# VectorE instead of Pool computes the lower weight parts during the selective scan of a hybrid decoder step

## What is computed

```python
def mamba_mixer(h, ssm_state, conv_state, in_w, conv_w, conv_b, dt_bias, a_log, d_skip, norm_w, out_w):
    z, xbc, dt = split(h @ in_w)
    xbc = silu(causal_conv(xbc, conv_w, conv_b))        # 4 taps
    xs, Bm, Cm = split(xbc)                             # 4 groups of 8 heads
    y, h_last = ssd_scan(xs * dt, dt * A, Bm, Cm, h0)   # chunks of 128 tokens
    y = (y + xs * d_skip) * silu(z)
    y = y * rsqrt(mean(y * y, by group) + eps) * norm_w
    return y @ out_w, h_last, new_conv
```

## Time and profile before

| | before |
|---|---|
| median of 3 runs | 2139.93 us (2133.59 to 2141.44) |
| profiled execution, its own time | 2141.42 us |
| its span in the trace | 2139.7 us |
| PE busy | 1987.8 us, 93% |
| VectorE, ScalarE, Pool busy | 38%, 33%, 45% |
| mean granted TensorE clock | 0.938 |
| chain of waits, by engine | PE 63%, issue 13%, DVE 9%, POOL 8%, ACT 5% |

### The profile page before, as it was taken

How to read it: one execution, slowest core, us unless ns; L and a number is a source line. 1 busy time by engine, 2 the same in 40 slices (tenths; PEclk the granted TensorE clock), 3 DMA queues, 4 the chain that set the end, 5 groups by cost and what they waited for, 6 DMA issues and landing times.

```text
span 2139.7 us, 36778 instructions
## 1 busy us (share of the span) xinstructions
PE 1987.8 (93%) x14824; PEld 1822.0 (85%) x14824; DVE 818.6 (38%) x1564; ACT 705.8 (33%) x1291; POOL 960.4 (45%) x685
## 2 busy tenths in 40 slices
PE   6989899979889998999999999989978999999997
PEld 5987887868788998999998998855547899999996
DVE  7373564746454210022233112267745622002134
ACT  4453553633133211122223113166634422112222
POOL 2445454454447532356453332344402565345552
PEclk9998999989998979999996998989999899999998
DMA  4211313122131216222221244350060122222221
GB/s 162 76 50 40 119 50 118 40 84 109 50 115 60 87 52 158 79 79 80 87 79 69 79 146 123 95 188 1 21 237 31 50 79 89 79 79 88 79 79 64
DMA packets 52629, 184.61 MB, mean 86 GB/s; under 512 B 7070, under 2 KB 11838, under 8 KB 50976
## 3 DMA queue, kind: packets, MB, share of 16 engines
q1 hardware_dynamic: 40272, 129.66, 18.3%
q0 software_dynamic: 9952, 50.08, 6.5%
q10 hardware_dynamic: 2288, 3.23, 0.4%
HBM read 166.59 MB, written 27.28 MB: 91 GB/s over the span
## 4 chain that ended last, share of the span: by engine, by line
PE 63%; issue 13%; DVE 9%; POOL 8%; ACT 5%; DMA 1%; ACTq 0%; POOLq 0%; SPq 0%; DVEq 0%
PE dense L1273 44%; POOL split L673 4%; PE dense L1596 3%; PE dense L1679 2%; PE dense L1636 1%; DVE tile L1815 1%; PE bS L1385 1%; PE bXM L1666 1%; POOL tile L767 1%; DMA o_sssm<-tile 1%; PE dense L1294 1%; POOL hid L792 1%; PE bXM L1447 1%; PE bXM L1392 1%; ACT tile L1111 1%
## 5 line engine op out<-in xcount | busy, mean ns | idle before, releaser
L1273 PE MATMUL dense<-xs,split 128*128 128x288 f32 x6848 | 987.0, 302 | 31.2 <-POOL split L673 9.1
L1273 PEld LDWEIGHTS dense<-xs,split 128*128 128x128 f32 x6848 | 950.4, 194 | 65.1 <-issue 45.4
L673 POOL TENSOR_TENSOR split<-ring,split 128x1024 fp32r<-128x1024 f32 x212 | 533.5, 2516 | 856.6 <-ACT split L919 834.5
L919 ACT ACTIVATE split<-ring 128x1024 fp32r<-128x1024 f32 x212 | 224.0, 1057 | 822.5 <-PE dense L1273 799.1
L1273 PE MATMUL dense<-hid,split 128*128 128x288 f32 x3072 | 416.7, 298 | 6.4 <-POOL split L673 6.4
L1273 PEld LDWEIGHTS dense<-hid,split 128*128 128x128 f32 x3072 | 415.1, 191 | 6.6 <-POOL split L673 6.6
L1827 DVE SCALAR_TENSOR_TENSOR tile<-tile,dense 128x576 f32<-128x576 f32 (+1 forms) x56 | 42.2, 754 | 421.7 <-PE dense L1273 421.7
L1997 DVE TENSOR_SCALAR sq<-dense 128x576 f32<-128x576 f32 x64 | 48.5, 758 | 310.4 <-PE dense L1273 310.4
L890 POOL TENSOR_SCALAR tile<-tile,tile,tile 128x128 f32<-128x128 f32 (+3 forms) x128 | 77.2, 617 | 81.4 <-DVE tile L2161 81.4
L1815 DVE SCALAR_TENSOR_TENSOR tile<-tile,tile,tile 128x512 f32<-128x512 f32 x72 | 87.6, 1217 | 42.4 <-ACT tile L1000 40.6
L792 POOL TENSOR_TENSOR hid<-sq,hid 128x576 f32 x64 | 76.9, 1202 | 0.0
(11 more groups left out here) (316 smaller groups left out, 2198.4 us busy)
## 6 DMA issues: line engine op xcount, KB each, us to landing
ring<-in_w SPq DMA_DIRECT2D x212, 512.0 KB, 3.3
tile<-in_state POOLq DMA_DIRECT2D x4, 2048.0 KB, 9.5
o_sssm<-tile POOLq DMA_DIRECT2D x4, 2048.0 KB, 7.5
tile<-in_cmp POOLq DMA_DIRECT2D x32, 256.0 KB, 3.2
tile<-in_win POOLq DMA_DIRECT2D x8, 1024.0 KB, 6.0
tile<-in_sel SPq DMA_DIRECT2D x32, 256.0 KB, 5.2
o_kv<-tile POOLq DMA_DIRECT2D x1, 3456.0 KB, 12.2
bskew<-bscr SPq DMA_DIRECT2D x1, 3072.0 KB, 23.0
```

Source lines behind the costliest of these rows:

```text
L673: pool.tensor_tensor(split[:, j, 1, :], ring[:, j, :], split[:, j, 0, :].bitcast(F32), ALU.subtract).then_inc(w_split, 1)
L919: act.activation(split[:, j, 0, :], ring[:, j, :], ACT.Copy).then_inc(w_hi, 1)
L1273: mm = pe.matmul(dense[:, 2 * par + h_, 0:HT], split[:, j, w, cols], v[:, kk, h_ * HT:(h_ + 1) * HT], start=kk == 0 and t == 0, stop=kk == ...
```

## The change

From the first tile on VectorE makes the lower parts of the scan. A stands behind the convolution (and norm, and residual) of its tile and ahead of the wait for y (`y_done`). B stands in the next tile, behind the mask L1878 and ahead of the product L1883; for the last tile it stands behind the loop. Each has a wait for `w_hi`, the first one also a wait until Pool has done its own 12. Pool gets one new wait behind the scan, until VectorE has made its last lower part, ahead of its next one.

```diff
@@ gpsimd, in the tiles
                 if n + 1 < len(TILES):
                     segment_rows(*TILES[n + 1])
-                if filler(g, c):
-                    split_lo(filler(g, c)[0] + 2)
                 if c == 3:
...
                     if g + 1 < MG:
                         load_states(g + 1)
-                if filler(g, c):
-                    split_lo(filler(g, c)[1] + 2)
...
+            pool.wait_ge(w_split, S_OUT[1] + 2)
             finish_los(0)
@@ vector
+            def split_lo(s):
+                if s == GB + 2:
+                    dve.wait_ge(w_split, s)
+                dve.wait_ge(w_hi, s + 1)
+                j = s % NSLOT
+                dve.tensor_tensor(split[:, j, 1, :], ring[:, j, :], split[:, j, 0, :].bitcast(F32),
+                                  ALU.subtract).then_inc(w_split, 1)
+
+            def split_before(n):
+                if n and filler(*TILES[n - 1][:2]):
+                    split_lo(filler(*TILES[n - 1][:2])[1] + 2)
...
                 dve.tensor_tensor(Gm[0:L, 0:L], bM[0:L, P:P + L], triu[0:L, c // 4, 0:L], ALU.mult
                                   ).then_inc(g_masked, 1)
+                split_before(n)
                 dve.wait_ge(g_masked, n + 1)
...
                     residual(B_OUT[0], 2 * c - 2, ALPHA, filler(g, c)[0] + 1)
+                if filler(g, c):
+                    split_lo(filler(g, c)[0] + 2)
 
                 dve.wait_ge(y_done, n + 1)
...
                 if c == 0 and g:
                     mean_square(g - 1)
+            split_before(len(TILES))
             mean_square(MG - 1)
```

## The result

The changed kernel takes 2102.02 us (median; 2100.64 to 2109.36) beside 2139.47 us for the kernel before on the same chip: a ratio of 0.984 (95% interval 0.981 to 0.986), 37 us less; the slowest run after lies 24 us under the fastest before. The profiled execution took 2102.03 us, its span is 2100.3 us (2139.7 before), its mean granted clock 0.946 (0.938 before).

A forecast was written before the change was run, and what follows sets the result against it. TensorE's waits in the scan for VectorE and Pool chains, with VectorE blocked by Pool's lower part, were taken as the bound. Terms 6.8 + 6.5 + 2.1 + 4.8 + 3.6 + 1 = 24.8 us less gave 2115 us, range 2107 to 2128.

The forecast's parts named there:

- The mechanism: In the scan, VectorE's two-operand SBUF work stands still while Pool's lower part runs; a tap takes 2.96 instead of 0.75 us.
- the group starts: Starts of groups 1 to 3: TensorE's waits for xdec shrink without Pool's B ahead of it, 4.8 us gained.
- (3, 1): Tile 1 of group 3: the norm takes 3.0 instead of 5.87 us; minus A, 1.7 us gained.
- the ordinary ends: Four tile ends with no norm behind: each stall of 2.2 us shrinks by 1.7, 6.8 us gained.
- four times 1.62 us of clock: Behind the four ordinary tile ends' stalls the clock stays high, 6.5 us gained.
- The rival by which the lock stays with Pool's other work: Pool's other work blocks the taps instead, tile ends keep their 2.2 us stalls: 2132 us; chance 0.13.
- the rival of a clock that stays low: Behind the shortened stalls the clock stays low, 6.5 us less gain: 2121.5 us; chance 0.2.
- A as pure addition: Taps long for another reason, A adds 1.2 us at some 16 tile ends: 2154 us; chance 0.08 with late ScalarE.
- c = 4: Tiles with c = 4: A and Pool's first multiplication collide at y's sum; 0 to 4.8 us gained, 1 taken.
- (3, 3): Tile 3 of group 3: y's lower parts take 3.0 instead of 4.91 us, 1.9 us gained; clock left out, up to 1.6.
- the norm tiles: Tiles c = 3 of groups 1 and 2: stalls at both ends shrink, together 2.1 us gained.
- A wrong sign that I had named: A wait of VectorE for ScalarE's split ahead of A would show the forecast wrong.

The follow-up runs named there:

- e4: Changed kernel, with idle subtractions on Pool (about 2.1 us, result unread) at A's old place in all 19 tiles: 2146.95 us.
- e7: Kernel before, all lower parts still on Pool, but A moved behind the update of the state: 2112.3 us.
- e1: Changed kernel with only A on VectorE; B stays with Pool at its old place: 2124.57 us.
- e2: Changed kernel with only B on VectorE; A stays with Pool at its old place: 2131.35 us.
- e5: Changed kernel, with idle subtractions on Pool at A's old place in the four c = 4 tiles only: 2114.31 us.
- e3: Kernel before, with Pool making the scan's lower parts for 8 of 1024 columns only, the rest left out: 2080.64 us.
- e8: Changed kernel with A, in c = 4 only, behind the second of the eight states instead of ahead of y: 2094.38 us.
- e6: Changed kernel with A behind the state update in every tile, in c = 4 behind the second of the eight states: 2083.46 us.
- e13: e6 with the norm's products in the norm tiles of groups 1 and 2 made for 8 of 576 tokens only: 2074.2 us.
- e12: Changed kernel with the norm's products in the norm tiles of groups 1 and 2 made for 8 of 576 tokens only: 2091.89 us.

## Why the prediction was right, and where it was wrong

**The mechanism** was right for the tile ends, the group starts and (3, 1). The taps are short, the subtraction takes 1.22 us in the median on VectorE and 1.29 in the mean (forecast 1.2), the ordinary ends and (3, 1) came out within 0.7 us of their terms, and four times 1.62 us of clock came back. The rival by which the lock stays with Pool's other work fell: two taps of 2.4 us and a few of 1.5 remain in the scan, but none at the ends that count. So did the rival of a clock that stays low (window of 1.00 above) and that of A as pure addition (e4 has it: there A and a blocked tap stand together, and the time is a little above that of before). The Trainium skill's warning ("Perfetto Trace Analysis", Optimizing Scalar/DVE Operations) that moves between these two engines might not help did not come true here: the runs show 37 us. e7 shows why the gain and the lock can both be right: what counts is what VectorE does while Pool reads.

**The step that failed is c = 4.** I priced it as a lock alone, 0 to 4.8 us, took 1, and gave the clock there no price, without a reason, though I had one for the ordinary ends. It gave 8.8 us. The collision that I expected did take place, in tile (1, 4) of the changed kernel:

```profile
306.54 1.23 DVE L1869 TENSOR_TENSOR split<-ring,split 128x1024 fp32r<-128x1024 f32 x1 [12.29 <-ACT split L916]
306.66 3.19 POOL L739 TENSOR_TENSOR tile<-tile,tile 128x512 f32<-128x512 f32 x2 [8.24 <-issue]
...
311.38 1.13 PE L1444 MATMUL bXM<-tile,tile 32*128 32x512 f32 x4 [2.00 <-DVE tile L1942]
```

A and the first two multiplications start together, and these take 3.19 instead of 2.04 us; y's gathering, behind A, starts at 307.68. The stall inside so falls only from 2.79 to 2.00 us: 2.4 us in three tiles, well inside the bounds that I gave. The other 6.4 us are clock (TensorE's busy time in these tiles, for the same instructions, falls from 93.7 to 87.7 us). Part of that looks like luck: (0, 4) alone gave 7.0 us, and in e1, e2, e4 and e5, with stalls no shorter than in the changed kernel, it took 29.7 to 31.7 us, between its two values of 33.95 and 26.97. That the clock had a price there could have been read from the trace of before. There, in the same tile, the twelve matmuls behind that stall take 3.25 us, where they take 1.87 at the full clock:

```profile
331.44 1.98 PE L1447 MATMUL bXM<-tile,tile 32*128 32x512 f32 x4 [2.79 <-DVE tile L1926]
333.36 3.25 PE L1273 MATMUL dense<-xs,split 128*128 128x288 f32 x12
...
342.81 1.87 PE L1273 MATMUL dense<-xs,split 128*128 128x288 f32 x12
```

A window over each of the three tiles (0.76 to 0.80) would have shown how much there was to win: in e3 the three tiles, at 1.00, are 24.5 us shorter, of which 5.0 us are the shorter stalls inside. With the clock's part as the upper end of this term the range would have reached below 2100. The low end itself was also added up too high: the forecast's terms, the clock of (3, 3) and c = 4 at its good end, off the lowest run shown, are 2133.6 - 24.8 - 1.6 - 3.8 = 2103 us, not 2107. The measured time lies below that too.

**(3, 3)** is the other term: I counted its stall alone, 1.9 us. The stall went from 3.72 to 1.57 (2.15 us), and the clock of the tile from 0.87 to 1.00, another 2.6 us; I had left this out, with 1.6 as its bound, the price of an ordinary end. These two terms, c = 4 and (3, 3), are 10.6 of the 13.1 us that the scan gained beyond the sum. The rest is small: the norm tiles 1.4 (their ends are 2.55 and 2.60 us long, forecast about 3), (0, 0) 1.1, the ordinary ends 0.7, the group starts 0.7 the other way.

**A wrong sign that I had named** was there: VectorE does wait for ScalarE's split ahead of A, 6.5, 12.3 and 11.1 us in the c = 4 tiles of groups 0 to 2 (under 1 us elsewhere), where it would have had to wait for TensorE anyway. What it costs there is the 1.2 us of A ahead of y, and with it the clock that e8 and e6 win back.

## What to carry to other kernels

Where a tap and an operation of Pool, both on SBUF, overlap on the chain that TensorE waits for, ask first for a moment at which VectorE reads PSUM or waits; moving the operation in time (e7) gave two thirds of what moving it to the other engine gave here, and with both (e6) nearly all of its cost is gone. Where a change shortens a stall of TensorE, price the clock behind it from a window over the whole stretch that follows, not only over the instructions up to the next dense block: in the c = 4 tiles the clock gave 6.4 us and the stall 2.4. Where the clock is borderline, one traced execution isn't enough to price it. And bound such a change with a run that leaves the work out before choosing its place.

## What the runs showed of the hardware

- In c = 4 the clock's share was larger than the stalls'. In the kernel before, stalls of 2.8 us inside c = 4 stood with a clock of 0.76 to 0.80 over 34 us, stalls of 1.1 us with at most 1.1 us ahead of the tile with 1.00 (e3, e13): 7 to 9 us a tile, of which the shorter stall itself is 1.7 us. It isn't a matter of length alone: with 3.97 us inside, tile (0, 4) of e5 had 0.94 over 30.4 us.
- In the executions traced, the stall ahead of a c = 4 tile and the one inside each took their part of its clock (the square above); the other runs of e12 and e8 show that the same kernel can come out either way.
- With idle work of about 3 us on Pool in each tile and nothing else changed, the kernel lost 45 us (e4 against after): an engine that TensorE does not wait for can set the time through the one that it does wait for.
